# Seven products of block sums in place of eight products of blocks in the gate and up stages of a Trainium2 decoder layer

## The reference, cut to what matters

```python
def swiglu(h, w_gate, w_up, w_down):
    return (jax.nn.silu(h @ w_gate) * (h @ w_up)) @ w_down
...
    f1 = swiglu(rms_norm(x, ffn1_pre_g[i]), ffn1_w_gate[i], ffn1_w_up[i], ffn1_w_down[i])
    x = x + FFN_RES_WEIGHT * rms_norm(f1, ffn1_post_g[i])
    m = token_mixer(...)
    x = x + rms_norm(m, mix_post_g[i])
    f2 = swiglu(rms_norm(x, ffn2_pre_g[i]), ffn2_w_gate[i], ffn2_w_up[i], ffn2_w_down[i])
    x = x + FFN_RES_WEIGHT * rms_norm(f2, ffn2_post_g[i])
    gate = jax.nn.sigmoid(rms_norm(x, ple_pre_g[i]) @ w_ple_gate[i])
    x = x + rms_norm(gate * (p[i] @ w_ple_proj[i]), ple_post_g[i])
```

## Time and profile before

| What | Value |
|---|---|
| median of 3 runs | 1078.94 us (1078.48 to 1079.03) |
| span of the profiled execution, first to last instruction | 1076.5 us |
| median less the span of the profiled execution | 2.4 us |
| busy share of the span: PE, PEld, DVE, ACT, POOL | 99%, 82%, 57%, 47%, 1% |
| matmuls | 4966 |
| read from HBM | 94.44 MB, 90 GB/s over the span |

### The profile page before, as it was taken

How to read it: one execution, slowest core, us unless ns; L and a number is a source line. 1 busy time by engine, 2 the same in 40 slices (tenths; PEclk the granted TensorE clock), 3 DMA queues, 4 the chain that set the end, 5 groups by cost and what they waited for, 6 DMA issues and landing times.

```text
span 1076.5 us, 15222 instructions
## 1 busy us (share of the span) xinstructions
PE 1062.5 (99%) x4966; PEld 887.9 (82%) x4966; DVE 618.6 (57%) x1043; ACT 510.1 (47%) x930; POOL 9.9 (1%) x33
## 2 busy tenths in 40 slices
PE   9999999999999999999998999999999999999997
PEld 7888888888888878888887888888888888888886
DVE  6454445444222689797979889544455445333655
ACT  6433333333222558686869746433333334333645
POOL 1000000000020000000000000000000000000000
PEclk9999999999999999999999999999999999999999
DMA  6333333333333332332312123333333334444002
GB/s 215 90 88 107 97 97 88 105 99 95 94 97 97 79 89 69 79 79 69 83 56 65 55 76 87 100 91 105 97 97 86 109 116 134 152 135 146 1 20 79
DMA packets 100948, 100.24 MB, mean 93 GB/s; under 512 B 7696, under 2 KB 83216, under 8 KB 100912
## 3 DMA queue, kind: packets, MB, share of 16 engines
q1 hardware_dynamic: 100496, 99.48, 31.7%
q10 hardware_dynamic: 416, 0.30, 0.1%
HBM read 94.44 MB, written 2.10 MB: 90 GB/s over the span
## 4 chain that ended last, share of the span: by engine, by line
PE 87%; DVE 6%; ACT 4%; issue 2%; DMA 0%; DVEq 0%; ACTq 0%
PE bank L1425 27%; PE bank L1426 27%; PE bank L1427 27%; PE bank L1737 1%; DVE w_r L931 1%; PE bank L1752 1%; DVE scratch L1323 1%; ACT scratch L669 0%; DVE big L1103 0%; PE bank L1701 0%; DMA gains<-in_gains 0%; ACT scratch L667 0%; DVE big L1100 0%; DVE acc L951 0%; DVE scratch L1094 0%
## 5 line engine op out<-in xcount | busy, mean ns | idle before, releaser
L931 DVE TENSOR_TENSOR w_r<-w_raw,w_r 128x512 fp32r<-128x512 f32 x332 | 225.4, 691 | 380.6 <-ACT w_r L510 374.9
L510 ACT ACTIVATE w_r<-w_raw 128x512 fp32r<-128x512 f32 x332 | 204.4, 628 | 403.8 <-PE bank L1427 400.7
L1425 PE MATMUL bank<-xg,w_r 128*128 128x512 f32 x890 | 349.2, 392 | 0.6 <-DVE scratch L1094 0.6
L1426 PE MATMUL bank<-xg,w_r 128*128 128x512 f32 x890 | 346.6, 389 | 0.0
L1427 PE MATMUL bank<-xg,w_r 128*128 128x512 f32 x890 | 346.5, 389 | 0.0
L1425 PEld LDWEIGHTS bank<-xg,w_r 128*128 128x128 f32 x890 | 167.1, 188 | 36.6 <-issue 1.4
L1427 PEld LDWEIGHTS bank<-xg,w_r 128*128 128x128 f32 x890 | 167.1, 188 | 35.2
L1426 PEld LDWEIGHTS bank<-xg,w_r 128*128 128x128 f32 x890 | 167.1, 188 | 34.5 <-issue 0.7
L1425 PE MATMUL bank<-big,w_r 128*128 (+2 forms) x420 | 163.5, 389 | 0.6 <-DVE big L1108 0.5
L1426 PE MATMUL bank<-big,w_r 128*128 (+2 forms) x420 | 162.6, 387 | 0.0
L1427 PE MATMUL bank<-big,w_r 128*128 (+2 forms) x420 | 162.6, 387 | 0.0
(11 more groups left out here) (168 smaller groups left out, 950.6 us busy)
## 6 DMA issues: line engine op xcount, KB each, us to landing
w_raw<-in_ffn_w_up SPq DMA_DIRECT2D x88, 256.0 KB, 2.8
w_raw<-in_ffn_w_down SPq DMA_DIRECT2D x88, 256.0 KB, 2.7
w_raw<-in_ffn_w_gate SPq DMA_DIRECT2D x87, 256.0 KB, 2.8
w_raw<-in_w_in SPq DMA_DIRECT2D x36, 256.0 KB, 3.1
scratch<-in_w_ple_gate SPq DMA_DIRECT2D x16, 256.0 KB, 3.4
w_raw<-in_w_in SPq DMA_DIRECT2D x24, 128.0 KB, 2.3
big<-big SPq DMA_DIRECT2D x24, 128.0 KB, 2.2
w_raw<-in_w_out SPq DMA_DIRECT2D x8, 256.0 KB, 2.8
```

What stands on the lines that cost most here:

```text
L510: act.activation(w_slot(0, slot, 0, 4 * P), w_raw[:, slot, :], ACT.Copy).then_inc(w_hi, 1)
L931: dve.tensor_tensor(w_slot(1, slot, 0, 4 * P), w_raw[:, slot, :], plain(w_slot(0, slot, 0, 4 * P)), SUB).then_inc(w_lo, 1)
L1425: pe.matmul(dst, w_hi_ap, m_hi, start=start, stop=False, skip_group_check=True)
L1426: pe.matmul(dst, w_lo_ap, m_hi, start=False, stop=False, skip_group_check=True)
```

## The change

The 11 steps of each gate/up stage become 3 plain steps, as before, and 8 fast steps (`fast_step`). A fast step makes the same 256 hidden features by the scheme of Strassen in Winograd's form. The work of a step is read as a product of 2 x 2 blocks: the input features in two halves of 512 (4 chunks each), the columns in gate (G) and up (U), the tokens in two halves of 256. In place of 8 products of blocks it takes 7 products of sums of blocks: their weights are G1, T1 = G1+U1, T2 = T1+U2, T3 = U1+U2, G2, T4 = T2+G2 and U2, where 1 and 2 are the halves of the input features. A block product is 4 chunks x 2 column tiles x 3 parts = 24 matmuls of 256 columns. The order is G1, T1, T2, T3, G2, T4, U2.

- The weights of a fast step come in four transfers of 512 KB. Sums T1 and T2 are made by VectorE, T3 and T4 by GpSimd (`lower_sums`), each an add of 128 x 1024 from SBUF, in place. Each of the 7 weight blocks (128 x 1024) is split in two parts by ScalarE and VectorE into a ring of 6 places, four of them in the old `xg` and two in the old `w_r`.
- The results are combined as they leave PSUM: G1's product is copied by ScalarE before G2 is added to its bank; VectorE makes four further reads of PSUM of 512 columns and one for the last up tile. Some products are accumulated into a bank that another one began.
- The moving blocks are sums of halves of the normalized x. They are made once in each gate/up stage: 8 multiplications by gain and factor (`scalar_tensor_tensor`, 128 x 512), 4 sums and 7 low parts on VectorE and 7 high parts on ScalarE (128 x 1024 each). They stand between the splits of units 12 to 21, in plain steps 1 and 2.
- The hidden values are kept in float32 in `scratch` and split in the down stage, one step ahead of their use (`hid_split_hi`, `hid_split_lo`, 128 x 1024 each). The up values are negated and the post gain is multiplied by -0.5 in place of 0.5.
- In f = 1 the matmul that sums the squares stands behind unit 8 in place of unit 10. The load and the split of `pT` are moved to the end of the down stage of f = 1. GpSimd clears the mixer's pads after unit 32 of the down stage in place of 24. The fast steps are written out and not looped.

The core of the diff:

```diff
+K_G1, K_T1, K_T2, K_T3, K_G2, K_T4, K_U2 = range(BLOCKS)
+BLOCK_BANK = [0, 1, 3, 2, 0, 2, 1]
+RING = [0, 1, 2, 3, 4, 5, 1, 2, 0, 3, 4, 1, 2, 5]
...
+            def lower_sums(f):
+                for q in range(FAST):
+                    at, raw = FAST * f + q, raw_set[q % 2]
...
+                    pool.wait_ge(block_sum, 2 * at + 1)
...
+                    pool.tensor_tensor(raw[RAW_U1], raw[RAW_U1], raw[RAW_U2], ADD).then_inc(block_sum_pool, 1)
+                    pool.wait_ge(block_lo, BLOCKS * at + K_T2 + 1)
...
+                    pool.tensor_tensor(raw[RAW_G1], raw[RAW_G1], raw[RAW_G2], ADD).then_inc(block_sum_pool, 1)
...
+                for q in range(FAST):
...
+                        up1(q - 1)
+                        block_split_lo(f, q, K_T3)
+                    block_split_lo(f, q, K_G2)
+                    if q:
+                        fast_hidden(q - 1)
+                    block_split_lo(f, q, K_T4)
+                    block_split_lo(f, q, K_U2)
+                    dve.wait_ge(block_used, used + K_T2 + 1)
+                    dve.wait_ge(g1_copied, at + 1)
+                    dve.tensor_tensor(u, sil[q % 2][:, 0, :], banks[3][:, :], SUB).then_inc(u_done, 1)
+                    if not last:
+                        block_split_lo(f, q + 1, K_G1)
...
+                    dve.wait_ge(block_used, used + K_T3 + 1)
+                    dve.wait_ge(u_done, at + 1)
+                    dve.tensor_tensor(up2, banks[2][:, :], u, ADD).then_inc(t_done, 1)
+                    dve.wait_ge(t_done, at + 1)
+                    dve.tensor_tensor(up2, banks[1][:, :], up2, ADD).then_inc(up2_done, 1)
+                    if not last:
+                        make_t1(f, q + 1)
+                        block_split_lo(f, q + 1, K_T1)
+                        make_t2(f, q + 1)
...
+                    dve.wait_ge(block_used, used + K_T4 + 1)
+                    dve.tensor_tensor(sil[q % 2][:, 1, :], banks[2][:, :], u, ADD).then_inc(gate2_done, 1)
+                    if not last:
+                        block_split_lo(f, q + 1, K_T2)
...
+            def fast_step(f, q):
+                at, banks = FAST * f + q, bank[4 * (1 - q % 2):4 * (1 - q % 2) + 4]
+                for k in range(BLOCKS):
+                    pe.wait_ge(block_lo, BLOCKS * at + k + 1)
...
+                    if k == K_G2:
+                        pe.wait_ge(g1_copied, at + 1)
+                    if k == K_T4:
+                        pe.wait_ge(t_done, at + 1)
+                    if k == K_U2:
+                        pe.wait_ge(up2_done, at + 1)
+                    place = RING[(BLOCKS * q + k) % len(RING)]
+                    opens = k <= K_T3
+                    for c in range(4):
+                        for a in range(2):
+                            w = slice(256 * c + P * a, 256 * c + P * a + P)
+                            last = product(banks[BLOCK_BANK[k]][:, 2 * P * a:2 * P * (a + 1)], ring[0][place][:, w],
+                                           ring[1][place][:, w], xc[0][k][:, c, :], xc[1][k][:, c, :],
+                                           opens and c == 0 and a == 0, c == 3)
+                    last.then_inc(block_used, 1)
```

More of the change, by code:

```diff
@@ L307, in load_up @@
                         step_unit(0, j)
[L308 to L309 removed]
+                    step(1)
+                    step(2)
                 else:
@@ L552, in up, with x_hi, hid_split_hi, split @@
+            def x_hi(f, j):
+                act.wait_ge(x_sum, 12 * f + X_SUM[j])
+                act.activation(xc[0][j], x_src[j], ACT.Copy).then_inc(xc_hi, 1)
+            def hid_split_hi(f, s, slot):
+                act.activation(hid[slot][0], hidden_f[:, ds(2 * s, 2), :], ACT.Copy).then_inc(hid_hi, 1)
             def up(f, pre_bank):
                 n = N_FFN1_PRE if f == 0 else N_FFN2_PRE
[L555 to L560, removed]
+                def split(u):
+                    split_hi(U_UP[f] + u, u % SLOTS, after=U_UP[f] + u - SLOTS + 1)
@@ L571, in up @@
-                if f == 0:
-                    step(0, first=True)
-                    with act.Fori(1, STEPS - 1) as s:
-                        step(s)
-                else:
[L576 to L579, removed]
+                        act.wait_ge(gate_out, 2 * (PLAIN * f + s) + a + 1)
+                        act.activation(plain_tmp[a], plain_tmp[a], ACT.Silu).then_inc(silu_done, 1)
@@ new lines, in up @@
+                if f == 0:
+                    split(10)
+                    factor(n, 0, pre_bank, D)
+                    split(11)
+                    hidden(0)
+                    for u in range(12, 20):
+                        split(u)
+                        for j in {13: (0,), 16: (1,), 17: (2, 3), 18: (4, 5), 19: (6,)}.get(u, ()):
+                            x_hi(f, j)
+                    hidden(1)
+                    split(20)
+                    split(21)
+                else:
+                    split(12)
+                    factor(n, 0, pre_bank, D)
+                    split(13)
+                    split(14)
+                    x_hi(f, 0)
+                    split(15)
@@ L580, in up @@
                     hidden(0)
-                    for j in range(12, 16):
-                        ahead(U_UP[1], 0, STEP_UNITS, j)
+                    for u in range(16, 20):
+                        split(u)
+                        for j in {17: (1,), 18: (2, 3), 19: (4, 5)}.get(u, ()):
+                            x_hi(f, j)
                     hidden(1)
-                    with act.Fori(2, STEPS - 1) as s:
-                        step(s)
-                step(STEPS - 1)
+                    split(20)
@@ L1071, in down @@
                         ahead(U_DOWN[f], s, 4, j)
+                hid_split_lo(f, 1, 1)
+                for j in range(4):
+                    ahead(U_DOWN[f], 0, 4, j)
+                with dve.Fori(0, BODY_STEPS // 2) as s2:
+                    step(2 * s2 + 1, 0)
+                    step(2 * s2 + 2, 1)
+                hid_split_lo(f, STEPS - 1, 0)
                 if f == 1:
```

420 lines of the change are left out of this document (328 added, 92 removed).

## The result

The changed kernel takes 1055.41 us (median of 4 runs, 1054.77 to 1055.76), the kernel before 1078.71 beside it: ratio 0.9785, 95% interval 0.9771 to 0.9799, so 23.3 us less. The forecast was 1054.3, range 1051.5 to 1066. The profiled execution took 1055.47 us with a span of 1053.7, so 1.8 us lie around the span.

The account below looks back on a forecast made before the run. TensorE, busy 99% of the span, was taken to bound the kernel. Span 1076.5 - 26.1 (products) + 1.5 (stall) = 1051.9, plus 2.4 beside the span, gives 1054.3 us; range 1051.5 to 1066.

Parts of the forecast that it names:

- The products: Fast steps: 168 matmuls at 0.1198 us take 20.13 us in place of 21.76; 26.1 us less over 16 steps.
- The loads: TensorE's weight loads in fast steps: 0.120 us apart, they keep the matmuls' pace and the clock stays at 1.00.
- The stall in f = 1: Before unit 22: moving blocks on VectorE stall TensorE 1.5 us, between 0 and 4.8.
- Around the span: Outside the profiled span: 2.4 us that the median has beside it, added to the span of 1051.9.
- GpSimd's add: Each weight sum on GpSimd in a fast step: 2.1 us, taken between 0.96 and 3.2.
- VectorE's room: Fast step: VectorE needs 14.3 us by spacing, 18.5 if GpSimd holds it wholly, still under TensorE's 20.13.
- smallest distance of 2.2 us, at T4: Order inside a fast step: VectorE's work is ready at least 2.2 us before TensorE needs it, least at T4; waits cost nothing.
- Rival A: Fast steps: GpSimd's adds hold VectorE, which sets the pace; step 20.7 us, 9 us lost, 1063; chance 0.13.
- each is started 8 us or more before its block is due: nothing on the path: GpSimd's two sums in a fast step: started early enough to add no time.
- B: Fast steps: VectorE held by GpSimd, counted at durations, needs 22.0 us a step; 1084, slower; chance 0.07.
- C: Fast steps: TensorE doesn't hold 0.1198 us a matmul over whole steps; 8 us lost, 1062; chance 0.08.
- D: Fast steps: late blocks eat 1.6 us in each step and the time stays at 1079; chance 0.02.

Follow-up runs that it names:

- Experiment 1: Kernel before, eight products kept, each 512-column matmul of gate/up steps 2 to 10 split into two of 256 columns: 1101.78 us, ratio 1.0216.
- experiment 4: Changed kernel with the last five low parts of the moving blocks in f = 1 moved behind the splits of units 19 to 23: 1052.89 us.
- Experiment 2: Changed kernel with all four weight sums of a fast step on VectorE, none on GpSimd: 1055.58 us, ratio to before 0.9786.
- experiment 3: Changed kernel with each of GpSimd's two adds of a fast step done twice in a row: 1110.93 us, ratio to before 1.0300.
- experiment 5: Changed kernel with all four weight sums of a fast step on GpSimd: 1063.09 us, ratio to before 0.9857.
- experiment 6: Changed kernel with all four sums on VectorE and the last moving-block low parts of f = 1 in later order: 1053.67 us, ratio to before 0.9770.
- experiment 7: Changed kernel with each GpSimd add followed by three fills of the same tile, which only write: 1058.93 us, ratio to before 0.9819.

## Why the prediction was right, step by step

**The products.** The main term stood at 26.1 us and is 25.6: the pace is 0.1200 and not 0.1198. Over 48 matmuls, the last hundredth of a microsecond in the two times is already 0.0002 each. Experiment 1 shows the two halves of the term by themselves.

**The loads** keep the pace and the clock stays at 1.00 in the window, as said.

**The stall in f = 1** was put at 1.5 us about unit 22, bounds 0 and 4.8; it is 2.3. The place and the cause (the moving blocks in VectorE's queue) are right, as experiment 4 shows by taking it away. The size is off since the sum followed one chain to one unit; TensorE also stalled at unit 20, 0.7 us, before VectorE got to unit 22. In f = 0 there is none, as said.

**Around the span** 2.4 us were taken, a median beside the span of another execution. In single executions it is 1.8: 1055.47 and 1053.7 for the changed kernel, and for the kernel before, timed beside the experiments, 1078.06 and 1076.3, 1079.13 and 1077.4. So the profiled execution before was itself some 0.6 us faster than the median one. Since the forecast took both from the same two numbers, it was in effect worked out from the median, and this misreading costs it nothing.

**The sum** therefore closes: 1078.9 - 26.1 + 1.5 = 1054.3 was forecast, 1078.7 - 25.6 + 2.3 = 1055.4 is measured. The difference is +0.5 (pace), +0.8 (stall) and -0.2 (the kernel before, timed again).

**GpSimd's add** is 2.4 us, with 2.1 taken between 0.96 and 3.2. The 2.3 us that the prediction estimated from the Trainium skill's figure for twice the columns ("GPSIMD Engine Reference", section 3.1) is nearer than the middle of the rows.

**VectorE's room is the step that was right only in its outcome.** The prediction had 14.3 us of work a step, 18.5 with a whole hold, so 1.6 free. Experiment 2 shows the work without hold, four sums included, at 17.25, so 15.0 with two, between the two ways of counting. The hold came and made 17.7, less than 18.5 since part of each add lies beside reads of PSUM and waits. What was left out is that VectorE also stands in order at low parts whose high part isn't there yet, 1.8 us a step, so that 0.5 to 0.7 us were free and not 1.6. "Near 75% busy" is 105.29 / 120 = 88% in the fast steps. The "smallest distance of 2.2 us, at T4" is right in place and nearly in size: it is 1.99, and experiments 3, 5, 6 and 7 all lose their time at T4. But a distance is a lead and not a room: with VectorE's order 0.35 us a step too long, experiment 7 had used it up after five steps. Rival A, given 0.13, was closer than that: its mechanism is real, and the step held with under a microsecond to spare. The cover was less than half of the 1.6 us that the prediction counted. That "each is started 8 us or more before its block is due: nothing on the path" costed the sums by GpSimd's time alone; in experiment 7 the sums are there 3 us later, well within the 8, and the kernel loses 3.5 us, since VectorE stands in order at T4's low part.

**The rivals.** A and B: the hold is shown (the changed kernel, experiment 3), but with two adds of 2.4 us it doesn't set the pace. C falls by 1344 matmuls at 0.1200 and by experiment 1. D falls by the trace.

What stays open: why the start differs by up to 0.5 us between executions of like code, and why the mixer stretch runs at the lower clock in some executions and not in others.

## What to carry to other kernels

Where TensorE sets the pace, a scheme with fewer products is worth its products less what the smaller matmuls lose, and both are read from the distance between matmuls in a row of the same width. The room of the helping engine isn't the step less its busy time: take off its waits in an order that can't be changed, and the hold by an engine that runs beside it; here 5.8 us on paper were some 0.6. And tell room from lead: a lead of 2 us hid an overload of 0.35 us a step for five steps, so a short stage would have shown none. Two adds a step given to GpSimd cost VectorE more by the hold (17.7 us a step) than making them (17.25), and paid only 0.8 us in the one step in which VectorE was behind. Last, TensorE at its lower clock isn't a cost by itself: in experiment 3 another engine's order set the step.

## What was not expected of the hardware

- A VectorE instruction held by GpSimd is shown as longer (2.38 to 3.42 us in place of 1.22), not as idle time before it; busy shares count the hold as work, and the count of instructions is needed to see it.
- The hold goes both ways. An add of GpSimd that starts while a VectorE instruction on two SBUF tiles runs is longer too: 3.26 us in place of 2.4 in experiment 3, in 30 of the 32 second adds of a pair. In the changed kernel the first add, at 66.35 us, takes 3.05, with a low part running from 65.93 to 67.15, and two of f = 1 take 2.51 and 2.68; the other 29 take 2.4.
- What the clock does after a wait of some 2 us isn't settled by the wait. In experiment 3 a wait of 2.1 us once in 23.8 us was followed by some 3 us at a granted clock of 0.50; in the mixer the same wait of 2.33 us was followed by 0.50 in the changed kernel and by 1.00 in the kernel before. Waits ahead of T4 of 0.7 us (experiment 6) and of 0.6 us, once 1.7 (experiment 5), were followed by a matmul distance of 0.12 again.
